# One step of a hybrid streaming encoder: a new order of mixer and last stage, and activations laid out by groups of four tiles

## The chip, the cores and the metric

The kernel runs on one core of one Trainium2 chip. The metric is device time in microseconds (us), the median of several executions. The engines of a core are TensorE (PE), VectorE (DVE), ScalarE (ACT), GpSimd (POOL) and SyncE (SP), which here only issues DMAs. Each runs its own instruction stream in order and waits on semaphores.

## What is computed

640 tokens (512 of a prompt, 8 streams of 16), model width 1024, float32:

```
h  = rmsnorm(x, norm1_g)
cb, cc, ch, q, k, v, rg, ga, gb = split(h @ w_in)        # w_in: 1024 x 9216
u  = cc * ch;  y_conv = cb * conv3(u)                    # causal, width 3
q, k = rope(q), rope(k) / 16                             # 4 heads of 256
o  = chunkwise_retention(q, k, v, state)                 # decay by head
y_ret = silu(rg) * rms_group_norm(o)
x  = x + (sigmoid(ga) * y_conv + sigmoid(gb) * y_ret) @ w_out
h2 = rmsnorm(x, norm2_g)
# PEER: 8 heads, 128 x 128 experts, top 16 of each head
s  = scores of h2 @ wq against two sets of 128 sub-keys; top 16 of each, top 16 of the sums
x  = x + sum over picked experts e: softmax(s_e) * gelu(u_tab[e] . h2) * v_tab[e]
y  = rmsnorm(x, final_g)
```

The outputs are y, the last two rows of u, and the new retention states.

## The kernel before, in words

Tokens lie in five tiles of 128 (`TT`). Products in full accuracy are made of three matmuls: each operand is split in a high part (ACT, `high_a`, L684) and a low part (POOL, `low`, L636).

*Start.* SP loads x; for each tile ACT squares and sums it (`norm_row`, L705), takes the square root (L708), DVE makes the factor with six small operations (`row_factor`, L973 to L978), ACT scales (`scale_rows`, L716), PE transposes (`turn_rows`, L1522), DVE and POOL split the result (`split_rows` L995/L996, `rows_low` L645). All this goes tile by tile.

*Mixer.* `w_in` comes in 72 column tiles through a ring of four buffers (`tile_in`, L460). PE's `product` (L1485 to L1487) makes 128 x 640 outputs with 48 matmuls of 320 columns. ACT copies them out (`out_of_psum`, L699). Tiles come in rounds of 8: four heads (q, q, k, k, v, v, rg, rg), then 8 of gb, then 8 conv rounds of 4 (cc, ch, cb, ga). Beside the round of head h runs the retention of head h - 1: PE's `retention_step` after each product (transposes L1534, scores L1541, outputs L1593, prompt state L1602, then `stream` for 8 streams, L1550 and L1560, the mean square L1617). DVE does `scores` (L1041, the kw products L1047), `rotate_q` and `rotate_k` (L1009 to L1014), `prompt_state` (L1069), `stream_state` (L1078), `outputs` (L1089 to L1099). In the gb round `gb_times` (L1104) stands in place of the rotations.

*Transposed table.* Beside the mixer the 128 tiles of `u_t` are loaded into two buffers (`turn_in`, L479), transposed by DVE (`turn`, L1022) and stored as `u_rows` (`turn_out`, L473). `turn_in(m)` waits until tile m - 2 is transposed. Written-out lists fix where these stand: `EARLY` and `TURN_IN` on SP, the `turn(...)` calls on DVE. SP issues weight tiles, u tiles, u rows and states in one order, and a waiting instruction holds back all behind it.

*w_out.* `by_token` (L1506 to L1508) adds eight parts into each of ten accumulators of 512 columns. Part i waits for the high and low mixer tile i (`m_ready`, set by L1203).

*Queries, up.* 48 query products (L1667), then 128 `up` tiles (L1707): the 384 tokens of the last three tiles (`TD`) against all 16384 experts, GELU by ACT (L872), stored to `acts` in DRAM, 1.5 KB per partition and tile. DVE does the retrieval and makes gates, which go to DRAM as `gates` by groups of four tiles. The first two token tiles go another way: for each of 256 token rows POOL gathers rows of `u_rows` and `peer_v` (L671; 14 slots), and DVE makes dots (L1346) and sums (L1364) in pairs (`pair_step`).

*Last stage (down).* For each group of four tiles SP loads gates and activations (`group_in`, L591 and L593) into two alternating buffers, and tiles of `peer_v` (`down_in`, L604) into a ring of eight. DVE multiplies (`weigh`, L1398), PE multiplies with the value tile: `down` (L1768), or for three of five tiles (`three(e)`) `down_three` (L1760 to L1762), which needs high parts by ACT (L935, L937) and low parts by DVE (`low_of_tile` L1405, `low_of_gated` L1411). In before, `low_of_gated(e - 1)` stands behind `weigh(e)`. At the end the five tiles are normed and stored.

Of the kernel before, what the change touches and what calls it, by code (L numbers as in the profile page):

```python
# [53 lines left out]
UP_BANKS = 2  # L54
AHEAD = 2
# [14 lines left out]
EARLY = 5  # L70
TURN_IN = (3, 3, 2, 3, 2, 2, 2, 1)
# [118 lines left out]
def build_program(nc, io):  # L190
    ctx = ExitStack()
    with ctx:
# [158 lines left out]
        acts = nc.dram_tensor("acts", [NKEY, P, TD], F32).ap()  # L351
# [43 lines left out]
        c_used = sem("c_used")  # L395
        m_ready = sem("m_ready")
# [58 lines left out]
        def _(sp):  # L455
# [34 lines left out]
            for u in range(GROUP):  # L490
                tile_in(u, io["w_in"][GROUP + u, :, :], 1)

# [89 lines left out]
            def group_in(g):  # L582
# [9 lines left out]
                src = acts[g * GROUP:(g + 1) * GROUP, :, :].rearrange("k p t -> p k t")  # L592
                sp.dma_start(al[:, g % 2, :, :], src).then_inc(al_loaded[g % 2], 16)  # L593
# [84 lines left out]
        def _(act):  # L678
# [126 lines left out]
            def conv_tile(ct, u, first=False):  # L805

                if u == 0 and not first:
                    act.wait_ge(c_used, ct)
                out_of_psum(c_in[:, u, :], u % 2, ACT.Sigmoid if u == 3 else ACT.Copy, ct * GROUP + (HEADS * 8 + KT + u))

            def conv_tiles(ct, first=False):
                for u in range(GROUP):
                    a = ct * GROUP + (HEADS * 8 + KT + u)
                    high_a((u + 2) % GROUP, a + 2, a + 2)
                    if first and u == 0:

                        act.wait_ge(gate_used, KT)
# [140 lines left out]
        def _(dve):  # L958
# [9 lines left out]
            def row_factor(which, tt):  # L968


                dve.wait_ge(rms_ready, which * TT + tt + 1)
                r_, t_, m_ = (t[:, tt:tt + 1] for t in (rstd, rms, ss))
# [5 lines left out]
                then(nc.vector.tensor_tensor(r_, r_, t_, ALU.mult), factor_ready, which * TT + tt + 1)  # L978
# [20 lines left out]
            for tt in range(TT + 1):  # L999
                if tt < TT:  # L1000
                    row_factor(0, tt)
                if tt:
                    split_rows(0, tt - 1, hf, g1)
# [29 lines left out]
            def scores(g, r):  # L1033
# [4 lines left out]
                for j in range(PT + 1):  # L1038
                    dve.wait_ge(att_done, g * 5 + (j + 1))
# [4 lines left out]
                    if j == 4:  # L1044
                        turn(0, 1, r, PER_HEAD)
                for s in range(PT):
                    then(nc.vector.tensor_scalar(kw[:, s, :], kv[:, s, 0:DK], key_decay(g, s), None, ALU.mult),  # L1047
                         kw_ready, g * 12 + (s + 1))
# [5 lines left out]
                turn(1, 2, r, PER_HEAD)  # L1054
# [59 lines left out]
            def head_round(h, first):  # L1114
# [24 lines left out]
            for t in range(4):  # L1139
                gb_times(t)  # L1140
                turn(n_gb + 3 + t, 1)
# [699 lines left out]
```

## Time and profile before

| what | us |
|---|---|
| median of three runs | 2345.77 |
| lowest, highest | 2332.7, 2359.89 |
| the profiled execution, its own time | 2338.41 |
| its span | 2336.6 |

Busy times are sums over one engine. "Idle" is time before an instruction in which its engine did nothing, with the name of what released it. The granted clock is TensorE's, as a share of full speed. Stages by the start of PE's work: products 33 to 713, w_out to 780, queries to 932, up to 1692 (gates beside it from 1466), down 1697 to 2328.

### The profile page before, as it was taken

How to read it: one execution, taken by the hardware profiler on the slowest of the kernel's cores; microseconds unless marked ns; L12 is line 12 of the kernel's file. 1: busy time of each engine (PE TensorE's matmuls, PEld its weight loads, DVE VectorE, ACT ScalarE, POOL GpSimd, SP SyncE). 2: the span in 40 equal slices, each digit the busy share in tenths (PEclk: the TensorE clock that was granted, in tenths of full speed). 3: DMA queues.
4: the chain of work that ended last, by engine and by line, in shares of the span. 5: the costliest groups of instructions: out<-in, count | busy, mean ns of one | idle time of the engine just before them, and what ended most of it. 6: DMA issues, size and time to landing. Idle time of an engine off the chain costs nothing.

```text
span 2336.6 us, 30091 instructions
## 1 busy us (share of the span) xinstructions
PE 2228.0 (95%) x10245; PEld 1663.9 (71%) x10245; DVE 1701.5 (73%) x3158; ACT 536.7 (23%) x1087; POOL 802.4 (34%) x606
## 2 busy tenths in 40 slices
PE   6999999899999999999999999999999999999998
PEld 5889989899997975655565655777655656656654
DVE  4576675567755287889979989988576777667676
ACT  3212222122222111121211211333222222122222
POOL 4322122123332005474564655111043343334340
PEclk9999999999999999999999999999999999999999
DMA  4898989989862459899999999787899999999993
GB/s 148 280 334 282 318 275 308 320 298 319 299 215 102 148 181 371 311 394 408 366 412 385 384 412 377 252 281 254 282 392 359 375 386 365 372 387 351 350 409 124
DMA packets 326436, 735.36 MB, mean 315 GB/s; under 512 B 30368, under 2 KB 179616, under 8 KB 326304
## 3 DMA queue, kind: packets, MB, share of 16 engines
q1 hardware_dynamic: 202080, 439.67, 52.5%
q0 software_dynamic: 73728, 268.47, 29.9%
q10 hardware_dynamic: 50496, 25.59, 3.6%
q8 instruction: 67, 1.10, 0.2%
q14 instruction: 65, 0.53, 0.1%
HBM read 604.04 MB, written 129.57 MB: 314 GB/s over the span
## 4 chain that ended last, share of the span: by engine, by line
PE 74%; DMA 12%; DVE 8%; issue 2%; SPq 2%; ACT 1%; POOL 0%; ACTq 0%; DVEq 0%; POOLq 0%
PE ps L1707 27%; PE ps L1768 8%; DMA b<-acts 8%; PE ps L1667 6%; PE ps L1485 5%; PE ps L1487 5%; PE ps L1486 5%; PE ps L1722 4%; PE ps L1760 3%; DMA b<-in_u_t 3%; PE ps L1762 3%; PE ps L1761 3%; PE ps L1560 1%; DVE b L1022 1%; PE ps L1550 1%
## 5 line engine op out<-in xcount | busy, mean ns | idle before, releaser
L1707 PE MATMUL ps<-b,b 128*128 128x384 f32 x2048 | 665.6, 486 | 0.0
L1707 PEld LDWEIGHTS ps<-b,b 128*128 128x128 f32 x2048 | 387.1, 190 | 263.1
L671 POOL DMA_INDIRECT b<-u_rows,b x256 | 255.1, 996 | 848.4 <-DVE b L1346 645.1
L671 POOL DMA_INDIRECT b<-in_peer_v,b x256 | 339.2, 1325 | 114.3 <-DVE ps L1364 66.9
L1485 PE MATMUL ps<-b,b 128*128 128x320 f32 x1152 | 366.0, 318 | 5.0 <-ACT b L699 4.4
L636 POOL TENSOR_TENSOR b<-b,b 128x1024 fp32r<-128x1024 f32 x80 | 195.3, 2445 | 490.5 <-ACT b L684 486.0
L1486 PE MATMUL ps<-b,b 128*128 128x320 f32 x1152 | 359.9, 312 | 0.0
L1487 PE MATMUL ps<-b,b 128*128 128x320 f32 x1152 | 359.7, 312 | 0.0
L1364 DVE SCALAR_TENSOR_TENSOR ps<-b,b,ps 128x1024 f32<-128x1024 f32 x252 | 323.2, 1283 | 46.2 <-ACT b L888 27.3
L1346 DVE CUSTOM_DVE_ANT_0 b<-b,b 128x1024 f32<-128x1024 f32 x256 | 312.4, 1220 | 21.3 <-DMA b<-u_rows,b 19.8
L1768 PE MATMUL ps<-b,b 128*128 128x512 f32 x648 | 286.1, 592 | 0.0
L1022 DVE STREAM_TRANSPOSE b<-b 128x1024 f32<-128x1024 f32 x128 | 157.3, 1239 | 168.4 <-DMA b<-in_u_t 163.5
L1760 PE MATMUL ps<-b,b 128*128 128x512 f32 x444 | 197.0, 444 | 37.8 <-DVE b L1411 37.7
L1485 PEld LDWEIGHTS ps<-b,b 128*128 128x128 f32 x1152 | 220.2, 191 | 6.5 <-issue 5.6
L1486 PEld LDWEIGHTS ps<-b,b 128*128 128x128 f32 x1152 | 220.0, 191 | 0.9
L1487 PEld LDWEIGHTS ps<-b,b 128*128 128x128 f32 x1152 | 219.6, 191 | 0.0
L1768 PEld LDWEIGHTS ps<-b,b 128*128 128x128 f32 x648 | 122.9, 190 | 135.1 <-issue 131.1
L1398 DVE TENSOR_TENSOR b<-b,b 128x384 f32<-128x384 f32 x128 | 71.8, 561 | 188.7 <-DMA b<-acts 172.7
L1762 PE MATMUL ps<-b,b 128*128 128x512 f32 x444 | 177.8, 400 | 0.0
L1761 PE MATMUL ps<-b,b 128*128 128x512 f32 x444 | 177.7, 400 | 0.0
L872 ACT ACTIVATE b<-ps 128x384 f32<-128x384 f32 x128 | 62.6, 489 | 486.2 <-PE ps L1707 480.0
L699 ACT ACTIVATE b<-ps 128x640 f32<-128x640 f32 (+1 forms) x72 | 50.7, 704 | 451.3 <-PE ps L1487 403.4
(158 smaller groups left out, 2585.8 us busy)
## 6 DMA issues: line engine op xcount, KB each, us to landing
b<-in_u_t SPq DMA_DIRECT2D x256, 512.0 KB, 6.1
u_rows<-b SPq DMA_DIRECT2D x512, 128.0 KB, 4.4
b<-in_peer_v SPq DMA_DIRECT2D x128, 512.0 KB, 8.9
b<-in_w_in SPq DMA_DIRECT2D x72, 512.0 KB, 5.5
b<-in_wq SPq DMA_DIRECT2D x48, 512.0 KB, 4.5
acts<-b SPq DMA_DIRECT2D x128, 192.0 KB, 7.8
gates<-b ACTq DMA_DIRECT2D x12, 2048.0 KB, 8.1
b<-gates SPq DMA_DIRECT2D x32, 768.0 KB, 9.6
```

The costliest lines, as they stand in the source:

```text
L636: nc.gpsimd.tensor_tensor(lo[u][:, :], raw[:, u, :], hi[u][:, :].bitcast(F32), ALU.subtract).then_inc(lo_ready, 1)
L671: nc.gpsimd.indirect_dma_start(slots[n % SLOTS][:, :], None, u_rows if kind == "u" else v_rows, bass.IndirectOffsetOnAxis(ap=row_id[:, r_ ...
L1346: nc.vector.tensor_tensor_reduce(up_row, up_row, h_row[:, r_ // P, :], 1.0, 0.0, ALU.mult, ALU.add, dots[:, r_ // PAIR % LINES, r_ % PAIR: ...
L1364: nc.vector.scalar_tensor_tensor(out, down_row, row_w[:, b % LINES, i:i + 1], had, ALU.mult, ALU.add).then_inc(row_done, 1)
L1485: nc.tensor.matmul(out, wa_hi[u][:, cols], h_hi[:, k, tok], start=(k == 0), stop=False)
L1486: nc.tensor.matmul(out, wa_hi[u][:, cols], h_lo[:, k, tok], start=False, stop=False)
L1487: last = nc.tensor.matmul(out, wa_lo[u][:, cols], h_hi[:, k, tok], start=False, stop=(k == KT - 1))
L1707: last = nc.tensor.matmul(ps[:, 2 + e % UP_BANKS, 0:TD], w[:, k * P:(k + 1) * P], h2[:, k, SD:T], start=(k == 0), stop=(k == KT - 1))
L1760: nc.tensor.matmul(out, p_hi[:, u, tok], v_hi[n][:, cols], start=(e == 0), stop=False)
L1761: nc.tensor.matmul(out, p_hi[:, u, tok], v_lo[n][:, cols], start=False, stop=False)
L1762: last = nc.tensor.matmul(out, p_lo[:, u, tok], v_hi[n][:, cols], start=False, stop=False)
L1768: last = nc.tensor.matmul(ps[:, 2 + 2 * i + dh, :], p32[:, e % GROUP, i * P:(i + 1) * P], w[:, dh * 512:(dh + 1) * 512], start=(e == 0), s ...
```

## The change

1. Start: all five tiles are squared first, one square root and one set of factor operations serve all, then the tiles are scaled.
2. The u tiles: 4 early ones are issued before the ninth weight tile instead of 5 behind it, and the lists on SP and DVE are new. In `scores` the kw products and two transposes come before the fourth score.
3. PE: of the 8 streams some stand between the halves of a product.
4. Conv: ACT waits for `cc_used` (cc and ch) and `c_used` (cb and ga) apart, and not for `gate_used`.
5. w_out: the first two accumulators take parts 0 to 6 side by side before part 7.
6. Last stage: `group_in(g + 1)` before the group's `down_in`, `low_of_gated(e)` in its own tile.
7. `acts` has the shape of a group: a partition's four tiles adjoin, so that a group is read in runs of 6 KB.

```diff
-EARLY = 5
-TURN_IN = (3, 3, 2, 3, 2, 2, 2, 1)
+BESIDE = 2
+EARLY = 4
+TURN_FIRST = (4, 2, 3, 2, 2, 2, 2, 1)
+TURN_IN = (2, 0, 2, 3, 4, 1, 3, 3)
...
-        acts = nc.dram_tensor("acts", [NKEY, P, TD], F32).ap()
+        acts = nc.dram_tensor("acts", [NE_GROUPS, P, GROUP, TD], F32).ap()
...
+            sp.wait_ge(xs_ready, TT)
+            for i in range(EARLY):
+                turn_in(i, first=True)
...
-                    if first and t == 0:
-                        sp.wait_ge(xs_ready, TT)
-                        for i in range(EARLY):
-                            turn_in(i, first=True)
-                    for i in range(TURN_IN[t]):
-                        n = sum(TURN_IN[:t]) + i
-                        turn_in(EARLY + n, 0 if first else h - 1, PER_HEAD)
+                    share = TURN_FIRST if first else TURN_IN
+                    for i in range(share[t]):
+                        turn_in(EARLY + sum(share[:t]) + i, 0 if first else h - 1, PER_HEAD)
...
-                    for j in ((3, 4), (5,), (6,), (7, 8))[u]:
+                    for j in ((2, 3), (4,), (5,), (6, 7))[u]:
...
-                sp.dma_start(tile_of(acts, e), spill[:, e % 2, :]).then_inc(a_stored[e % 2], 16)
+                sp.dma_start(acts[e // GROUP, :, e % GROUP, :], spill[:, e % 2, :]).then_inc(a_stored[e % 2], 16)
...
-                src = acts[g * GROUP:(g + 1) * GROUP, :, :].rearrange("k p t -> p k t")
-                sp.dma_start(al[:, g % 2, :, :], src).then_inc(al_loaded[g % 2], 16)
+                src = acts[g, :, :, :].rearrange("p k t -> p (k t)")
+                sp.dma_start(al[:, g % 2, :, :].rearrange("p k t -> p (k t)"), src).then_inc(al_loaded[g % 2], 16)
...
                 if g + 1 < NE_GROUPS:
+                    group_in(g + 1)
                     for u in range(GROUP):
                         down_in((g + 1) * GROUP + u)
-                    group_in(g + 1)
...
-                norm_row(0, tt)
-                if tt:
-                    scale_rows(0, tt - 1, xs)
-            high_a(0, 0, 0, False)
-            scale_rows(0, TT - 1, xs)
+                nc.scalar.activation(ps[...], x[:, tt, :], ACT.Square, accum_out=ss[:, tt:tt + 1]).then_inc(sum_done, 1)
+            act.wait_ge(sum_done, TT)
+            nc.scalar.activation(rms[:, :], ss[:, :], ACT.Sqrt, bias=eps[:, 0:1], scale=1.0 / D).then_inc(rms_ready, TT)
+            for tt in range(TT):
+                scale_rows(0, tt, xs)
+                if tt == 1:
+                    high_a(0, 0, 0, False)
...
-                if u == 0 and not first:
-                    act.wait_ge(c_used, ct)
+                if u in (0, 2) and not first:
+                    act.wait_ge(cc_used if u == 0 else c_used, ct)
...
-                        act.wait_ge(gate_used, KT)
...
                 for j in range(PT + 1):
+                    if j == 3:
+                        for s in range(PT):
+                            then(nc.vector.tensor_scalar(kw[:, s, :], ...), kw_ready, g * 12 + (s + 1))
+                        turn(0, 2, r, PER_HEAD)
...
-                    if j == 4:
-                        turn(0, 1, r, PER_HEAD)
-                for s in range(PT):
-                    then(nc.vector.tensor_scalar(kw[:, s, :], ...), kw_ready, g * 12 + (s + 1))
...
-                turn(1, 2, r, PER_HEAD)
...
                 rotate_q(h)
-                turn(3, 2, h, PER_HEAD)
+                turn(2, 2, h, PER_HEAD)
                 rotate_k(h)
                 prompt_state(g, first)
-                turn(5, 1, h, PER_HEAD)
-                for s in range(STREAMS):
+                stream_state(g, 0)
+                done = 4
+                for s in range(1, STREAMS):
                     stream_state(g, s)
-                    turn(6 + s, 1, h, PER_HEAD)
+                    n = 2 if s in (3, 5, 7) else 1
+                    turn(done, n, h, PER_HEAD)
+                    done += n
...
-            for t in range(4):
-                gb_times(t)
-                turn(n_gb + 3 + t, 1)
+            gb_times(0)
+            turn(n_gb + 2, 1)
+            gb_times(1)
+            turn(n_gb + 3, 1)
+            gb_times(2)
+            turn(n_gb + 4, 1)
+            gb_times(3)
             prompt_state(HEADS - 1, False)
-            turn(n_gb + 7, 1)
...
                 if three(e):
                     low_of_tile(e)
-                if e and three(e - 1):
-                    low_of_gated(e - 1)
+                    low_of_gated(e)
...
+                    if hv == 0:
+                        between()
...
+                for i, pair in parts[:-1]:
+                    ready(i)
+                    for n in range(BESIDE):
+                        add(n, i, pair)
+                ready(e_)
+                for n in range(10):
+                    if n >= 4:
+                        pe.wait_ge(acc_added, stage * 10 + (n - 3))
+                    for i, pair in parts if n >= BESIDE else parts[-1:]:
+                        last = add(n, i, pair)
...
-                for s in {4: range(2), 5: range(2, 5), 6: range(5, 8)}.get(t, ()):
+                for s in {4: (0, 1), 5: (3,), 6: (5,)}.get(t, ()):
                     stream(g, s)
...
+            def streams_inside(g, t):
+                for s in {5: (2,), 6: (4,), 7: (6, 7)}.get(t, ()):
+                    stream(g, s)
```

## Rows read from the trace of the kernel before

**Rows 1.** The page, part 1: busy us, share of span, instructions of each engine.

```profile
PE 2228.0 (95%) x10245; PEld 1663.9 (71%) x10245; DVE 1701.5 (73%) x3158; ACT 536.7 (23%) x1087; POOL 802.4 (34%) x606
```

**Rows 2.** Windows by stage; columns: stretch, length, busy, clock, DMA share, GB/s.

```profile
0.00:60.00 60.00, 37.18 (x204) 33.76 (x205) 24.14 (x52) 22.67 (x31) 25.68 (x20) 1.00 0.42 154
60.00:500.00 440.00, 409.32 (x2575) 385.24 (x2574) 272.24 (x295) 97.57 (x132) 91.78 (x38) 0.96 0.89 299
932.00:1466.00 534.00, 534.00 (x1726) 319.44 (x1725) 489.17 (x1109) 99.15 (x303) 296.00 (x252) 1.00 1.00 382
1697.00:2300.00 603.00, 570.40 (x1913) 367.22 (x1914) 434.28 (x597) 139.49 (x308) 238.60 (x206) 0.98 0.95 368
...
1820.00:1880.00 60.00, 56.98 (x195) 36.32 (x195) 44.58 (x64) 14.91 (x33) 26.50 (x24) 1.00 1.03 409
```

**Rows 3.** Waits of PE over the whole span: us, times, longest.

```profile
PE ps L1760 <- DVE b L1411: 37.7, 14, 5.4
PE ps L1560 <- DVE b L1069: 16.5, 4, 8.8
...
PE ps L1485 <- ACT b L699: 4.4, 1, 4.4
PE ps L1506 <- DVE b L1203: 4.4, 1, 4.4
PE ps L1534 <- ACT b L737: 4.2, 1, 4.2
PE ps L1541 <- DVE b L1041: 2.8, 1, 2.8
```

**Rows 4.** Windows just behind waits: first of six, 723, first of five.

```profile
112.50:119.00 6.50, 6.50 (x16) 3.73 (x16) 2.40 (x3) 2.00 (x4) 1.90 (x1) 0.63 0.87 291
...
723.00:730.00 7.00, 6.93 (x20) 5.55 (x21) 0.69 (x1) 0.00 (x0) 0.00 (x0) 0.62 0.03 9
...
1774.00:1782.00 8.00, 7.88 (x21) 5.93 (x22) 8.00 (x12) 1.74 (x3) 3.46 (x3) 0.65 0.98 367
```

**Rows 5.** Last stage: timeline of VectorE at tile 7; its longest wait, 1697 to 2300.

```profile
1732.24 0.56 DVE L1398 TENSOR_TENSOR b<-b,b 128x384 f32<-128x384 f32 x1 [11.60 <-DMA b<-acts]
1732.71 0.55 DVE L1411 TENSOR_TENSOR b<-b,b 128x384 fp32r<-128x384 f32 x1
...
DVE b L1398 <- DMA b<-acts: 153.5, 23, 11.6
```

**Rows 6.** Timeline: VectorE in round 2; PE's waits for L1069, rounds 1 and gb.

```profile
220.94 0.29 DVE L1041 TENSOR_TENSOR b<-ps,b 128x128 f32<-128x128 f32 x1 [7.06 <-PE ps L1541]
...
223.08 3.17 DVE L1047 TENSOR_SCALAR b<-b,b 128x256 f32<-128x256 f32 x4
...
241.25 1.25 DVE L1022 STREAM_TRANSPOSE b<-b 128x1024 f32<-128x1024 f32 x1 [2.41 <-DMA b<-in_u_t]
...
157.50 1.10 PE L1560 MATMUL ps<-b,b 128*128 128x256 f32 x4 [0.75 <-DVE b L1069]
...
444.64 1.62 PE L1560 MATMUL ps<-b,b 128*128 128x256 f32 x3 [8.83 <-DVE b L1069]
```

**Rows 7.** Timeline of PE: first w_out matmul, first of its last part.

```profile
713.50 0.50 PE L1506 MATMUL ps<-b,b 128*128 128x512 f32 x1 [0.79 <-ACT b L699]
...
723.07 0.77 PE L1506 MATMUL ps<-b,b 128*128 128x512 f32 x1 [4.42 <-DVE b L1203]
```

**Rows 8.** DMA issues, page part 6: KB each, us to landing.

```profile
b<-gates SPq DMA_DIRECT2D x32, 768.0 KB, 9.6
b<-acts SPq DMA_DIRECT2D x32, 768.0 KB, 14.5
```

**Rows 9.** Timeline, first 62 us: ACT scaling tiles 2 and 3, VectorE's first u transpose.

```profile
17.22 1.15 ACT L716 ACTIVATE b<-b,b 128x1024 f32<-128x1024 f32 x1 [2.51 <-DVE b L978]
...
22.16 1.15 ACT L716 ACTIVATE b<-b,b 128x1024 f32<-128x1024 f32 x1 [2.43 <-DVE b L978]
...
59.66 2.43 DVE L1022 STREAM_TRANSPOSE b<-b 128x1024 f32<-128x1024 f32 x2 [24.58 <-DMA b<-in_u_t]
```

More of the change, by code:

```diff
@@ L395, in build_program @@
         c_used = sem("c_used")
+        cc_used = sem("cc_ch_used")
         m_ready = sem("m_ready")
@@ L966, in _, with row_factor @@
             nc.vector.memset(eps[:, :], EPS).then_inc(eps_ready, 1)
-            def row_factor(which, tt):
-                dve.wait_ge(rms_ready, which * TT + tt + 1)
-                r_, t_, m_ = (t[:, tt:tt + 1] for t in (rstd, rms, ss))
+            def row_factor(which, tt, n=1):
+                dve.wait_ge(rms_ready, which * TT + tt + n)
+                r_, t_, m_ = (t[:, tt:tt + n] for t in (rstd, rms, ss))
                 line.then(nc.vector.reciprocal(r_, t_))
@@ L977, in row_factor @@
                 line.then(nc.vector.tensor_scalar(t_, t_, -0.5, 1.5, ALU.mult, ALU.add))
-                then(nc.vector.tensor_tensor(r_, r_, t_, ALU.mult), factor_ready, which * TT + tt + 1)
+                nc.vector.tensor_tensor(r_, r_, t_, ALU.mult).then_inc(factor_ready, n)
+                dve.wait_ge(factor_ready, which * TT + tt + n)
             def split_rows(which, tt, hf_, gain):
@@ L998, in _ @@
             dve.wait_ge(consts, 16 * 2)
[L999 to L1003, printed above, removed]
+            row_factor(0, 0, TT)
+            for tt in range(TT):
+                split_rows(0, tt, hf, g1)
             def rotate(h, src, dst, n):
@@ L1173, in conv_round @@
                 line.then(nc.vector.tensor_tensor(ub[:, 2:2 + PROMPT], cc[:, 0:PROMPT], ch[:, 0:PROMPT], ALU.mult))
-                line.then(nc.vector.tensor_tensor(uv[:, :, 2:], streams_of(cc[:, PROMPT:T]), streams_of(ch[:, PROMPT:T]), ALU.mult))
+                nc.vector.tensor_tensor(uv[:, :, 2:], streams_of(cc[:, PROMPT:T]), streams_of(ch[:, PROMPT:T]),
+                                        ALU.mult).then_inc(cc_used, 1)
+                dve.wait_ge(cc_used, ct + 1)
                 line.then(nc.vector.tensor_copy(uv[:, :, 0:2], sconv[:, ds(ct, 1), :].rearrange("p o (b s) -> p (o b) s", b=STREAMS)))
@@ L1470, in _, with product @@
         def _(pe):
-            def product(u, par, n, a, wait_evac=True, rows_from=None):
+            def product(u, par, n, a, wait_evac=True, rows_from=None, between=lambda: None):
                 pe.wait_ge(lo_ready, n + 1)
@@ L1493, in by_token, with add @@
                 between = list(between)
-                for n in range(10):
+                parts = list(enumerate(zip(lhs, rhs)))
+                e_ = len(parts) - 1
+                def add(n, i, pair):
                     tt, dh = n // 2, n % 2
-                    if not (first and n < 4):
-                        pe.wait_ge(acc_added, stage * 10 + (n - 3))
                     out = ps[:, acc_bank(n, odd), :]
@@ L1501, in by_token @@
                     cols = slice(dh * 512, (dh + 1) * 512)
-                    for i, ((lh, ll), (rh, rl)) in enumerate(zip(lhs, rhs)):
-                        e_ = i == len(lhs) - 1
-                        if n == 0:
-                            ready(i)
-                        nc.tensor.matmul(out, lh[:, tok], rh[:, cols], start=(i == 0), stop=False)
-                        nc.tensor.matmul(out, ll[:, tok], rh[:, cols], start=False, stop=False)
-                        last = nc.tensor.matmul(out, lh[:, tok], rl[:, cols], start=False, stop=e_)
+                    (lh, ll), (rh, rl) = pair
+                    nc.tensor.matmul(out, lh[:, tok], rh[:, cols], start=(i == 0), stop=False)
+                    nc.tensor.matmul(out, ll[:, tok], rh[:, cols], start=False, stop=False)
+                    return nc.tensor.matmul(out, lh[:, tok], rl[:, cols], start=False, stop=(i == e_))
+                for i, pair in parts[:-1]:
[8 more added lines that the diff above has]
+                        last = add(n, i, pair)
                     last.then_inc(acc_done, 1)
@@ L1527, in _, with head_tile @@
                 turn_rows(0, tt, xs)
-            def head_tile(h, t, first=False):
-                product(t % GROUP, t % 2, h * 8 + t, h * 8 + t, not (first and t < 2), 0 if first and t == 0 else None)
+            def head_tile(h, t, first=False, between=lambda: None):
+                product(t % GROUP, t % 2, h * 8 + t, h * 8 + t, not (first and t < 2), 0 if first and t == 0 else None,
+                        between)
             def turn_kv(tt):
```

43 lines of the change are left out of this document (25 added, 18 removed).

## The prediction

> **What bounds the kernel now.** I read the page's engine shares first [rows 1]: TensorE (PE) is busy 2228.0 of 2336.6 us, so all idle time of PE together is 108.6 us. This caps what a reordering can give, apart from the clock. The stage windows [rows 2] say where it lies: 22.8 us in the first 60, 30.7 between 60 and 500 (retention heads), nothing in the up stage (534 of 534 busy), 32.6 in the last stage from 1697 to 2300. The list of PE's waits [rows 3] names what ends it: 37.7 us, 14 times, on `low_of_gated` of VectorE (L1411); 16.5 on `prompt_state` (L1069); 4.4 on ACT's copy out of PSUM (L699); 4.4 on the last low part of the mixer's product (L1203); 4.2 on L737; 2.8 on L1041. To each longer wait belongs a second price [rows 4]: the granted clock falls to its half level (1.2 of 2.4 GHz), and PE's next matmuls run there. Busy time times (1 - clock) is that loss: the first of six between 112 and 500 costs 6.5 x 0.37 = 2.4, the six 2.4, 1.7, 2.0, 2.6, 1.9 and 1.6, sum 12.2; the one at 723 costs 2.7; of five in the last stage the first costs 2.8, the others 1.7 each, sum 9.6.
>
> **Last stage: what the change removes.** The pattern repeats 13 times [rows 5]: tile 7 is the last of its group and one of the `three` tiles. VectorE has its v_lo by 1720, then goes to `weigh(8)`, which waits 11.60 us for the DMA of the next group's activations; only behind it stands `low_of_gated(7)` (L1411), for which PE waits. Two edits hit this, each enough by itself. First, `low_of_gated(e)` comes before `weigh(e + 1)`. It now waits for ACT's p_hi (about 0.5 us of ACT), beside which VectorE's 1.21 us of v_lo runs, so I charge 0; at worst 0.5 a tile, with VectorE busy 434 of 603 us [rows 2], which its lead of three tiles absorbs. Second, `group_in(g + 1)` leaves SP before the four `down_in` of that group. These wait until PE is through tile 4g - 1; the group's own wait (`p_ready`) is met about four tiles earlier. PE needs about 4.4 us a tile (561 over 128, below), so the load starts some 17 us earlier, against VectorE's waits for it of 11.6 at most once the stage runs [rows 5]. What queues behind SP's wait are four value tiles; they keep five tiles, 22 us, to land.
>
> The layout alone: the activations' DMA takes 14.5 us from issue to landing, the gates' of equal size, already in 6 KB runs, 9.6 [rows 8]. Both leave together, so the gap of 4.9 is in part queueing; the layout gives 0 to 4.9 us of latency a group, hidden now either way. The stores keep their runs.
>
> Ideal gain: waits 37.7 - 5.4 (the first, at 1697, where the stage waits for its first loads and not for the order) = 32.3, plus 9.6 of clock, plus 0.5 at the start (L1411 one `weigh` earlier) = 42.4. What may take it back is DMA: 368 GB/s x 603 us = 222 MB at a share of 0.95. In 561 us they need 396 GB/s. The kernel shows 409 for 60 us, and 382 with PE never idle in the up stage [rows 2]. At 409 the bytes take 543 us and PE stays the bound; at 382 they take 581, and 22 is gained. I take **34**, nearer to the ideal since 409 was reached in this very stage.
>
> A rule speaks against this: the Trainium skill, "DMA: Bandwidth & Descriptors" (Specifications), gives about 358 GB/s as the HBM limit of a core. By it these bytes need 620 us and this part would gain nothing. The 409 of [rows 2] is above it, so the measurement decides, and I give it only part of the DMA rival.
>
> **Heads.** PE waits for `prompt_state` 8.8 us in the gb round and 0.75 in round 1 [rows 6]; the list's 16.5 [rows 3] leaves 6.9 for rounds 2 and 3. In front of it VectorE still transposes for `u_rows`, and one transpose waits for its own load (2.41 us). After: the four kw products (3.2 us) and two transposes (2.4) stand between scores 2 and 3, where VectorE now idles 7.06 us [rows 6]; four transposes instead of five precede `prompt_state`, in the gb round five instead of seven. `rotate_k` then waits only for its tile. That is what round 1 shows already, with a stall of 0.75 [rows 6]. So 6.9 falls to 1.5, and their clock cost (4.6) goes; 8.8 + 1.9 go. Gain 5.4 + 4.6 + 10.7 = 20.7, bounds 8 and 22.
>
> Round 1 (4.2 + 2.8, clock 4.1): ACT's copy waits because weight tiles queue in SP behind transposes; VectorE got its first u tile only at 59.66, after 24.58 us of idling [rows 9], since SP issued it after the ninth weight tile. Now it is issued after the eighth, one product or about 7 us earlier (PE's 24 x 2 matmuls at about 0.145), more than either wait. Gain 11.1, bounds 4 and 11.1. The first conv tile (4.4 + 1.6): ACT no longer waits for `gate_used`, gain 6.0, bounds 3 and 6. PE's other, short waits in the heads stay. The streams moved into and behind the products are the same matmuls; where VectorE is late, two adjacent streams wait one 0.7 us operation, -2 at worst. `cc_used` splits a wait that PE does not feel in the conv rounds: 0, bounds 0 and 1.
>
> Sum 37.8. Against it: DMA share is 0.89 over 440 us [rows 2], and the same bytes in 402 us make 0.97. I hold 6 back and take **32** (bounds 13 and 38).
>
> **w_out.** PE had 21 matmuls to issue before `m_ready(8)`, 713.50 to 718.65, then waited 4.42 [rows 7]. With BESIDE = 2 it has 42, at 0.235 each 9.9 us, to 723.4, past the 723.1 at which the product comes. The wait and 2.7 of clock go: 7.1, I take **7** (bounds 4 and 7).
>
> **Start.** One square root and one set of six factor operations for all tiles replace five. They stand in the chain from one scaled tile to the next, 4.94 us (17.22 to 22.16) [rows 9]. Without them I estimate 3.3, so 1.6 saved for each of four tiles. But no scaling starts until the fifth x tile has landed and been squared; four squares, each about the 1.15 us of a scaling of the same size, come first, some 5 us. GpSimd's `low`, 2.4 us, now slows the chain too. 6.4 - 5 - 2.4 is -1, and bare arithmetic is no better than that here: I take **0** (bounds -3 and +3). What stands behind PE's end stays.
>
> **Sum.** 34 + 32 + 7 + 0 = 73. The profiled execution took 2338.4 us (span 2336.6): 2265. The three plain runs have a median of 2345.8, 7 above, and spread over 27; I give two thirds of the 7: **2270 us**.
>
> **Rivals.** A: DMA becomes the bound of the last stage. For it: share 0.95 now, 1.03 in a stretch. Against it: GpSimd's row loads have 14 slots of slack. The stage gains 22 or, at the 375 GB/s near today's mean, 11: 2282 to 2293. B: the u transposes stay bound by their loads in the heads (share 0.97), and stalls come back at other places; 32 falls to 13: 2289. Both together 2305. C, slower: SP stands at `p_ready` before `group_in(g + 1)` with four value tiles behind it. If VectorE is late (rows of retrieval between the weighs), these are late for PE in every group. It decides where `weigh` trails so far that more than the 22 us are used; to lose over 1% it must eat 73 and 24 more, 3.2 us in each of 31 groups. 3.5 each gives 2378. Against it: VectorE is free over a quarter of the stage. D: the stalls merely move, since PE then waits for p_ready of the next group's first tile: the change doesn't do what it says in the last stage; only 39 come from the rest: 2306.
>
> Chances: forecast 0.60, A 0.14, B 0.11, A with B 0.05, D 0.05, C 0.05. All but C, and half of D and of A with B by noise, lie over 1% below 2345.8. A measurement of this kernel tells about 1% from no change. So faster 0.88, within 1% 0.07, slower 0.05. Range: the ideal terms (42 + 38 + 7 + 3 = 90) give 2248; up to A with B, 2308.
>
> **What would show it.** PE's wait on L1411 falls from 37.7 to under 10, VectorE's on the acts DMA from 153.5 to under 35; the last stage is 590 to 602 long instead of 630, at over 385 GB/s. L1069 ends waits of under 4 us in all; no wait on L1203 over 1; the first u transpose is near 53. Wrong if the last stage stays over 620 us, if PE waits there on weight or value DMAs, or if the mixer ends (first w_out matmul) later than 690.

## The result, and the profile after

| | us |
|---|---|
| before, median of 4 runs measured beside the changed kernel (lowest, highest) | 2349.89 (2332.70, 2359.89) |
| after, median of 4 runs | 2273.33 (2269.06, 2288.35) |
| ratio, with its 95% interval | 0.9693 (0.9617 to 0.9769) |
| the profiled execution of after, its own time | 2269.06 |
| forecast, range | 2270, 2248 to 2308 |

The total is as forecast; its parts are not. Stage lengths from the start of PE's first instruction in each stage, in the profiled executions:

| stage | before | after | difference | forecast |
|---|---|---|---|---|
| start | 33.6 | 32.9 | -0.7 | 0 |
| mixer | 679.9 | 663.8 | -16.1 | -32 |
| w_out | 66.5 | 59.6 | -6.9 | -7 |
| queries | 152.8 | 151.2 | -1.6 | none |
| up | 764.4 | 765.3 | +0.9 | none |
| last stage | 630.4 | 585.4 | -45.0 | -34 |
| behind PE's end | 9.0 | 9.1 | +0.1 | 0 |
| span | 2336.6 | 2267.3 | -69.3 | -73 |

The mixer gave half of its term (15.9 us less than forecast) and the last stage a third more (11.0 more). The two errors largely cancel, so that the total came so near is in part luck.

From the page of after, the engines' busy times and the chain that ended last. PE's share was 2228.0 us of a longer span [rows 1]; it is now 97%.

```profile
span 2267.3 us, 30061 instructions
...
PE 2207.6 (97%) x10245; PEld 1653.6 (73%) x10245; DVE 1689.2 (75%) x3134; ACT 538.3 (24%) x1083; POOL 806.9 (36%) x606
...
PE 87%; DVE 4%; DMA 4%; issue 3%; POOL 1%; SPq 1%; ACT 1%; another core or an unknown queue 0%; ACTq 0%; DVEq 0%; POOLq 0%
PE ps L1735 28%; PE ps L1796 12%; PE ps L1695 6%; PE ps L1500 5%; PE ps L1499 5%; PE ps L1501 5%; PE ps L1788 5%; PE ps L1790 5%; PE ps L1789 5%; PE ps L1750 4%; DMA b<-in_u_t 3%; POOL b L638 1%; PE ps L1519 1%; PE ps L1520 1%; PE ps L1521 1%
```

The chain of before, by engine and by line:

```profile
PE 74%; DMA 12%; DVE 8%; issue 2%; SPq 2%; ACT 1%; POOL 0%; ACTq 0%; DVEq 0%; POOLq 0%
PE ps L1707 27%; PE ps L1768 8%; DMA b<-acts 8%; PE ps L1667 6%; PE ps L1485 5%; PE ps L1487 5%; PE ps L1486 5%; PE ps L1722 4%; PE ps L1760 3%; DMA b<-in_u_t 3%; PE ps L1762 3%; PE ps L1761 3%; PE ps L1560 1%; DVE b L1022 1%; PE ps L1550 1%
```

Before, the read of the activations was 8% of the chain; after, it is no longer in the list. The loads of the u tiles were 3% and still are.

What PE waits for in after: line waited for, us in total, times, longest.

```profile
PE ps L1546 <- ACT b L718: 15.5, 1, 15.5
PE ps L1559 <- DVE b L1094: 15.3, 3, 5.8
PE ps L1788 <- DVE b L1426: 5.6, 1, 5.6
PE ps L1546 <- DVE b L1002: 5.1, 8, 1.3
PE ps L1566 <- DVE b L1050: 3.8, 1, 3.8
```

The first row, 15.5, belongs to the start (ACT scaling the first tile): there, in before, PE waited 11.1 us for ACT and 11.2 for the split, now 15.5 and 5.1. L1426 is `low_of_gated`, L1411 in before. Its 14 waits [rows 3] are one, the stage's own start. `prompt_state` (16.5 before) is down to 0.7, and the waits on ACT's copy (4.4), on L737 (4.2) and on the last low part of the product (4.4) are gone. But the second row is new in size: before, PE waited 2.6 us for that line (the last operation of the retention's mean square, L1091 there); now it is 15.3, once each at the start of rounds 2 and 3 and of the gb round (5.8, 5.8 and 3.7).

The stages as windows of after, to be read beside [rows 2]: us, busy time of PE, PEld, DVE, ACT and POOL, granted clock, DMA share, GB/s.

```profile
60.00:500.00 440.00, 420.19 (x2675) 398.97 (x2674) 271.95 (x295) 105.26 (x139) 97.67 (x41) 0.97 0.92 304
907.00:1440.00 533.00, 532.63 (x1719) 318.10 (x1718) 489.30 (x1109) 98.81 (x302) 298.28 (x252) 1.00 1.00 384
1673.00:2230.00 557.00, 557.00 (x1910) 360.74 (x1911) 436.83 (x596) 140.64 (x308) 240.98 (x206) 1.00 0.99 398
```

In the last stage PE has no idle time in 557 us, while the DMAs move 398 GB/s: PE is full and no DMA wait of PE is left. By the Trainium skill, "DMA: Bandwidth & Descriptors" (Specifications), a core's HBM limit is about 358 GB/s; the same page (Bandwidth) has about 358 as what each core gets when both cores of an HBM domain stream, and more for a core alone. The measurement, 398, agrees with the second statement, and not with the first as a limit for this one-core kernel.

**The new wait, in the rows.** VectorE around 280 us in after (start, duration, line, operation, in brackets the idle time before it and its releaser), then PE's instruction that waited.

```profile
280.19 1.25 DVE L1026 STREAM_TRANSPOSE b<-b 128x1024 f32<-128x1024 f32 x1 [5.80 <-DMA b<-in_u_t]
281.36 0.71 DVE L1081 SCALAR_TENSOR_TENSOR b<-b,b,ps 128x512 f32<-128x512 f32 x1
282.85 1.25 DVE L1026 STREAM_TRANSPOSE b<-b 128x1024 f32<-128x1024 f32 x1 [0.79 <-DMA b<-in_u_t]
285.51 1.25 DVE L1026 STREAM_TRANSPOSE b<-b 128x1024 f32<-128x1024 f32 x1 [1.41 <-DMA b<-in_u_t]
286.68 4.11 DVE L1092 RECIPROCAL b<-b 128x640 f32<-128x640 f32 x1
290.82 2.04 DVE L1093 TENSOR_TENSOR b<-b 128x640 f32<-128x640 f32 x1
292.89 0.82 DVE L1094 SCALAR_TENSOR_TENSOR b<-ps,b 128x640 f32<-128x640 f32 x1
```

```profile
293.86 0.87 PE L1559 MATMUL ps<-b,b 128*128 128x128 f32 x3 [5.79 <-DVE b L1094]
```

A transpose for `u_rows` waits 5.80 us for its load and holds the last `stream_state` (281.36), then two more transposes, each with a late load (0.79 and 1.41), hold the reciprocal (286.68). Behind it come 7 us of arithmetic on PE's path. In all VectorE lost 8.0 us to loads here, and PE waited 5.79. The granted clock falls behind these waits to 0.76, 0.71 and 0.54 over some 6 us (1.5, 1.8 and 2.9 us lost), so this one line costs 12.7 us more wait than before and 6.2 of clock: 18.9.

### The profile page after: what moved, and what is told of

It is laid out like the page before. It is cut to its first block, busy times and chain, and to the rows that moved or that the text cites. A ratio compares the mean times of both kernels' runs of the same rounds, so it can differ in the third digit from the quotient of the medians.

```text
span 2267.3 us, 30061 instructions
## 1 busy us (share of the span) xinstructions
PE 2207.6 (97%) x10245; PEld 1653.6 (73%) x10245; DVE 1689.2 (75%) x3134; ACT 538.3 (24%) x1083; POOL 806.9 (36%) x606
## 4 chain that ended last, share of the span: by engine, by line
PE 87%; DVE 4%; DMA 4%; issue 3%; POOL 1%; SPq 1%; ACT 1%; another core or an unknown queue 0%; ACTq 0%; DVEq 0%; POOLq 0%
PE ps L1735 28%; PE ps L1796 12%; PE ps L1695 6%; PE ps L1500 5%; PE ps L1499 5%; PE ps L1501 5%; PE ps L1788 5%; PE ps L1790 5%; PE ps L1789 5%; PE ps L1750 4%; DMA b<-in_u_t 3%; POOL b L638 1%; PE ps L1519 1%; PE ps L1520 1%; PE ps L1521 1%
## 5 line engine op out<-in xcount | busy, mean ns | idle before, releaser
L1796 PE MATMUL ps<-b,b 128*128 128x512 f32 x648 | 286.1, 592 | 0.0
L1788 PE MATMUL ps<-b,b 128*128 128x512 f32 x444 | 194.7, 438 | 5.6 <-DVE b L1426 5.6
L1789 PE MATMUL ps<-b,b 128*128 128x512 f32 x444 | 174.2, 392 | 0.0
L1790 PE MATMUL ps<-b,b 128*128 128x512 f32 x444 | 174.1, 392 | 0.0
```

Of the source, the lines that this page charges most:

```text
L1788: nc.tensor.matmul(out, p_hi[:, u, tok], v_hi[n][:, cols], start=(e == 0), stop=False)
L1789: nc.tensor.matmul(out, p_hi[:, u, tok], v_lo[n][:, cols], start=False, stop=False)
L1790: last = nc.tensor.matmul(out, p_lo[:, u, tok], v_hi[n][:, cols], start=False, stop=False)
L1796: last = nc.tensor.matmul(ps[:, 2 + 2 * i + dh, :], p32[:, e % GROUP, i * P:(i + 1) * P], w[:, dh * 512:(dh + 1) * 512], start=(e == 0), s ...
```

## Experiments on the last stage

Here and below the stage lengths are the main reading. The reason is the up stage, in which no edit changes more than where the activations are stored: over all profiled executions of this study it was 764 to 767 us long in five and 776 to 789 in nine. Of the totals only those of several runs are given with an interval.

Each stage length is of one profile. How far a stage varies without an edit to it, the other runs show: the mixer of before was 679.9 to 684.4 us long in five profiles, that of after 663.8 and 662.4; w_out 65.6 to 66.8 in the old order and 59.5 or 59.6 in the new one; the last stage of after 585.1 to 586.5 in seven profiles, that of before 630.4 and 627.6. So before's 679.9 is the shortest of its five, and the mixer's gain is 16 to 22 us rather than exactly 16.1.

**`low_of_gated` in its own tile's step**, in the kernel before:

```diff
                 if three(e):
                     low_of_tile(e)
-                if e and three(e - 1):
-                    low_of_gated(e - 1)
+                    low_of_gated(e)
```

> The kernel before with one edit: low_of_gated(e) stands in tile e and not behind weigh(e + 1). Theory 1 (PE waited only because this product stood behind a weigh that waits for the next group's activations): PE's wait on it falls from 37.7 us to the first one, 5 to 6; the last stage is 588 to 595 long instead of 630.4; VectorE still waits over 100 us for the activations. Theory 2 (the late load is what counts, and the stall moves to the next tile): PE then waits as much before the first tile of each next group, the stage stays over 615. The mixer is as before, 680 +- 3.

**The group's read ahead of the value tiles**, in the kernel before:

```diff
                 if g + 1 < NE_GROUPS:
+                    group_in(g + 1)
                     for u in range(GROUP):
                         down_in((g + 1) * GROUP + u)
-                    group_in(g + 1)
```

> The kernel before with one edit: group_in(g + 1) is issued before the four value tiles of that group. Theory 1 and theory 2 both: VectorE's wait for the activations falls from 172.7 to the one at the stage's start (about 20), PE's on L1411 to 5 to 6, the stage to 585 to 592. Rival (DMA is the bound of this stage at over 390 GB/s): the load is earlier but waits stay on value or row loads, and the stage is over 600. The rival that SP's wait in front of the value tiles starves PE: PE waits on DMAs of peer_v.

**The layout alone**, in the kernel before:

```diff
-        acts = nc.dram_tensor("acts", [NKEY, P, TD], F32).ap()
+        acts = nc.dram_tensor("acts", [NE_GROUPS, P, GROUP, TD], F32).ap()
...
-                src = acts[g * GROUP:(g + 1) * GROUP, :, :].rearrange("k p t -> p k t")
+                src = acts[g, :, :, :].rearrange("p k t -> p (k t)")
```

> The kernel before with one edit: the layout of the activations by group, read in 6 KB runs. If short runs make the load slow: its time from issue to landing falls from 14.5 us to about 10, VectorE's waits for it from 172.7 to 90 or less, PE's on L1411 from 37.7 to 10 to 20, and the stage shortens by 15 to 30 us. If the 4.9 us over the gates' load are queueing behind it: the latency stays over 13, and the stage within 5 us of 630.

**All three in the kernel before:**

> Kernel before with all three edits of the last stage (the low part of the gated tile in its own tile's step, the group's read issued ahead of the value tiles, activations by group of four in DRAM), its heads and its w_out stage untouched. Each of the three alone left a last stage of 593.2, 586.2 and 596.7 us, the whole change one of 585.4. Theory, each removes the same stalls and the three don't add up: last stage 584 to 588 here, one PE wait of 5 to 7 us at its start, mixer 678 to 685 and w_out 66 to 67 as before, so the last stage's 45 us don't need the new order of the mixer. Rival, part of the 45 comes from what the mixer or w_out edit leaves behind (the two low parts or the clock at the start): last stage 590 or more.

Measured:

| | last stage, us | PE on `low_of_gated` | VectorE on the acts DMA |
|---|---|---|---|
| before | 630.4 | 37.7, 14 times | 172.7, 24 times |
| `low_of_gated` moved | 593.2 | 7.3, 6 times | 149.8, 23 times |
| read first | 586.2 | 6.7, once | 20.6, once |
| layout alone | 596.7 | 14.8, 10 times | 145.6, 25 times |
| the three together | 585.6 | 5.2, once | 19.4, once |
| after | 585.4 | 5.6, once | 19.7, once |

One wait of 19 to 21 us in the last column, and one of 5 to 7 in the column before it, belong to the stage's first loads. Without the former, before has 153.5 us in 23 waits [rows 5].

The total of the layout alone was 2321.52 us (4 runs), ratio 0.9888 (0.9849 to 0.9927). The first two, one run each, took 2315.81 and 2317.51 us, beside 2350.35 (7 runs) for before, both with a long up stage (778 and 782 us); the three together 2300.24 beside 2343.43. In the last of these the mixer (682.1) and w_out (66.8) are those of before: the 45 us need nothing of the other edits.

VectorE's waits, longest kind first, with `low_of_gated` moved (from 1710 us on, so without the first wait):

```profile
DVE b L1398 <- DMA b<-acts: 129.9, 22, 11.3
```

and with the read issued first, where only the stage's first wait is left:

```profile
DVE b L1398 <- PE ps L1762: 65.1, 42, 3.1
DVE b L1398 <- PE ps L1768: 60.2, 27, 4.6
DVE b L1398 <- DMA b<-acts: 20.6, 1, 20.6
```

These two fences say what 153.5 us of waiting by VectorE were worth. In the first kernel it still waits 129.9 us for the same DMA, and PE waits 7.3 on `low_of_gated`: what PE needs is no longer behind that wait. In the second the wait itself is gone, and VectorE waits for PE, as an engine with time to spare should. Either removes the stall. The layout removes no cause; VectorE's waits are 28.3 us less in sum (from 1700 us on):

```profile
DVE b L1398 <- DMA b<-acts: 125.2, 24, 11.5
```

PE's waits fell with them by 22.9. The run was expected to shorten the stage by 15 to 30 us and to halve VectorE's waits; it gave 33.7 and 16% less (172.7 to 145.6). The trace has no landing time for this read. Worked out from the timelines, from its issue to the `weigh` that had waited for it, the median of the waits longer than 6 us is 15.9 us in before and 13.0 here, so the read lands some 3 us earlier; what part of this is the length of the runs and what part queueing is not shown.

The single edits gave 37.2, 44.2 and 33.7 us, the three together 44.8: they overlap almost wholly.

**The old layout and `BESIDE` = 1 in the kernel after:**

```diff
-BESIDE = 2
+BESIDE = 1
...
-        acts = nc.dram_tensor("acts", [NE_GROUPS, P, GROUP, TD], F32).ap()
+        acts = nc.dram_tensor("acts", [NKEY, P, TD], F32).ap()
```

> The changed kernel with two parts undone that lie in different stages: the old layout of the activations, and BESIDE = 1 (one accumulator of w_out before the last mixer tile). If the new order already hides the loads, the last stage stays within 2 us of 585.4; if the layout's lower DMA cost is what let PE run, it is over 595. w_out is 66 to 67 us long instead of 59.6, with a wait of 4 to 5 us on the last low part and some 3 us of half clock behind it.

The last stage took 586.6 us, 1.2 more than in after and 0.1 above the spread of the new order: with it the layout is worth next to nothing. The total of this one run was 2299.23, with an up stage of 786. w_out took 66.8, which is before's 66.5, and its wait came back:

```profile
PE ps L1519 <- DVE b L1218: 4.4, 1, 4.4
```

So `BESIDE` = 2 is the whole of w_out's gain, in which the wait of 4.4 stands with the clock behind it.

## Experiments on the mixer

**The streams placed as before**, in the kernel after:

```diff
-                for s in {4: (0, 1), 5: (3,), 6: (5,)}.get(t, ()):
+                for s in {4: range(2), 5: range(2, 5), 6: range(5, 8)}.get(t, ()):
...
-                for s in {5: (2,), 6: (4,), 7: (6, 7)}.get(t, ()):
+                for s in ():
```

> The changed kernel with PE's streams where they were before (none between the halves of a product). Theory S (stream 7 now comes 4 to 5 us before the head's end, so that the state update behind it, and the square root that waits for it, are late): the waits of PE on L1094 fall from 15.3 us to 3 or less, and the mixer from 663.8 to 648 to 655. Theory T (the transposes on VectorE ahead of the reciprocal, with late loads, set it, wherever the streams stand): 10 us or more of it stays.

Mixer 671.5 us, 7.7 more than after; total of one run 2298.03. The wait grew, as theory T had it:

```profile
PE ps L1559 <- DVE b L1094: 21.1, 3, 8.0
```

The placing of the streams inside the products is thus a gain (by one profile on each side), and not the cause of the new wait.

**The last three transposes of the streams moved behind the mean square**, in the kernel after:

```diff
-                    n = 2 if s in (3, 5, 7) else 1
+                    n = 2 if s in (3, 5) else 0 if s >= 6 else 1
                     turn(done, n, h, PER_HEAD)
                     done += n
-                outputs(g, lambda: turn(14, 2, h, PER_HEAD))
+                outputs(g, lambda: turn(11, 5, h, PER_HEAD))
```

> The changed kernel with three transposes of each head round (behind streams 6 and 7) moved behind L1094. Theory T: VectorE reaches the reciprocal when the square root is there, the waits on L1094 fall from 15.3 to under 4 us, the mixer by 10 to 17 us with the clock, the time by 0.4 to 0.7%. Theory S: the wait falls by less than half. Rival (the loads are bound by DMA and the stall only moves): new waits of PE on scores or on weights of the same size, mixer within 4 us of 663.8.

```profile
PE ps L1566 <- DVE b L1050: 22.2, 4, 7.6
PE ps L1618 <- DVE b L1050: 4.1, 3, 1.9
PE ps L1559 <- DVE b L1094: 2.8, 3, 1.3
```

The aimed-at wait is gone, 15.3 to 2.8, and a larger one stands at the next thing that PE needs of VectorE, the scores of the next head (L1050), in front of which seven transposes now stand instead of four. The mixer was to become 10 to 17 us shorter by theory T and to stay within 4 us of 663.8 by the rival; it became 17.6 us longer, 681.4 us. Theory T was right on the wait and wrong on its worth, and the rival right that the stall moves. The total was 2302.14 us (4 runs), ratio to before 0.9783 (0.9714 to 0.9853). Both edits together:

> The changed kernel with both edits: streams where they were, three transposes behind L1094. Theory T: as a_turns within 3 us. Theory S: as a_streams. If each is half of it: mixer 645 to 650, below either alone.

Mixer 681.6 us, within 3 us of the edit alone, as theory T had it; L1050 23.4 us, total 2299.04 (4 runs), ratio 0.9786 (0.9726 to 0.9846). Moving the transposes moves the wait.

**The loads of the u tiles left out**, once in after, once in before:

```diff
-                sp.dma_start(u_in[m % 2], tile_of(io["u_t"], r * per + m)).then_inc(u_loaded[m % 2], 16)
+                if first and m < 2:
+                    sp.dma_start(u_in[m % 2], tile_of(io["u_t"], r * per + m)).then_inc(u_loaded[m % 2], 16)
...
-                    dve.wait_ge(u_loaded[i % 2], r * (per // 2 * 16) + 16 * (i // 2 + 1))
+                    dve.wait_ge(u_loaded[i % 2], 16)
```

> The changed kernel without the loads of the u tiles after the first two: the transposes and stores work on the same two tiles, so the rows of the table and the first two token tiles of the output are other numbers. Some 63 MB less are read beside the mixer. If late loads are behind the waits on L1094 and on the first round's score: both are gone or under 1 us each time, and the mixer is 645 to 650. If it is the order alone (streams, square root, reciprocal): waits of 3 us or more stay in each round.

> Kernel before with the loads of the u tiles left out but for the first two (the transposes run on old contents, so the table rows are other numbers; the stores stay). The same was done to the kernel after, where the mixer stage fell from 663.8 to 638.6 us. Theory 1, the new order is worth what the sum said and late loads took half of it back: without loads the difference between the two orders is about 32 us, so this kernel's mixer stage stays near 671 (668 to 675), only 5 to 12 below its 679.9, with the waits on the prompt state (L1069, 16.5) and the other old ones still there. Theory 2, the loads cost both orders the same and the new order is worth 16 with or without them: mixer near 655 (652 to 658). Theory 3, the old waits are themselves late loads passed on: mixer below 648, and the new order is worth under 10 once no load is late. Last stage 630 as before in all.

PE's waits between 60 us and the mixer's end, first after without loads, then before without loads:

```profile
PE ps L1560 <- DVE b L1095: 2.6, 3, 1.2
PE ps L1520 <- ACT b L702: 0.8, 1, 0.8
```

```profile
PE ps L1561 <- DVE b L1070: 9.4, 4, 4.7
PE ps L1486 <- ACT b L700: 4.5, 1, 4.5
PE ps L1535 <- DVE b L1092: 2.6, 3, 1.2
PE ps L1507 <- ACT b L700: 0.8, 1, 0.8
```

| mixer, us | with the loads | without | the loads cost |
|---|---|---|---|
| before | 679.9 | 659.7 | 20.2 |
| after | 663.8 | 638.6 | 25.2 |
| difference | 16.1 | 21.1 | |

The totals, one run each, were 2269.11 and 2325.87 us; the first had an up stage of 787 us, which hides the gain of its mixer. Of the theories for the second run the first (671) and the third (under 648) fall; 659.7 lies just above the second's 652 to 658. The new wait of after comes from the loads: without them the line is back to 2.6. But the old stalls came in good part from the loads as well: `prompt_state` 16.5 to 9.4, and the 4.2 and 2.8 of [rows 3] vanish without any change of order. The new order is worth 21 us without the loads and 16 to 22 with them, and the loads cost both orders 20 to 25 us. Leaving them out takes away more than their lateness: SP's time for issuing them, and a third of the DMA traffic of the mixer (289 and 296 GB/s before the edit, 197 and 204 with it). These runs do not tell the three apart.

## Two attempts to make the loads less late

SP in after around the late transpose at 280.19. Each row is a run of DMA issues.

```profile
266.86 0.37 SPq L482 DMA_DIRECT2D b<-in_u_t  x1
267.33 2.81 SPq L476 DMA_DIRECT2D u_rows<-b  x4
270.40 0.37 SPq L527 DMA_DIRECT2D b<-in_dec  x1
270.97 0.41 SPq L527 DMA_DIRECT2D b<-in_dec_s  x1
271.47 0.38 SPq L527 DMA_DIRECT2D b<-in_gq  x1
272.15 0.33 SPq L463 DMA_DIRECT2D b<-in_w_in  x1
272.67 0.33 SPq L482 DMA_DIRECT2D b<-in_u_t  x1
273.11 2.93 SPq L476 DMA_DIRECT2D u_rows<-b  x4
276.24 0.51 SPq L482 DMA_DIRECT2D b<-in_u_t  x1
```

The buffer of the load at 272.67 was free at 270.49 (a transpose from 269.24, 1.25 long); three tables and a weight tile were issued first. The next buffer was free at 272.25, but the load left at 276.24, behind the four stores of a turned tile, 2.93 us of issue. The first load landed 7.5 us after its issue, where the median of its kind is 5.6.

**Loads in pairs, ahead of the stores and tables**, in the kernel after, rounds 2 to 4 (SP's list for tiles 3 and 4 of the head; the tables go behind tile 4's turns):

```diff
+    [("in", 8), ("in", 9), ("out", 6), ("out", 7), ("in", 10), ("out", 8), ("in", 11), ("in", 12)],
+    [("out", 9), ("out", 10), ("in", 13), ("out", 11), ("in", 14), ("in", 15), ("out", 12), ("out", 13)],
```

> Kernel after, only the order in which SyncE issues things in rounds 2 to 4 of the heads is changed: where VectorE makes two transposes in a row, the two loads that follow them are issued one behind the other and the eight stores behind both (now load, four stores of some 0.7 us each, load, four stores); two loads go ahead of the three tables and of the weight load that stood in front of them; the tables go one tile later. Theory late loads by SyncE's issue order (in the trace of after the load for the transpose at 280.19 went out at 272.67, 2.2 us after its buffer was free, the next one at 276.24, 4 us after): VectorE's waits on u tiles between 60 and 500 us fall from 102.9 to under 85, PE's wait on L1094 from 15.3 to under 8, the mixer stage from 663.8 to 652 to 660, the total 5 to 10 us below after. Rival, the DMA queues' share sets it (0.92 in that stretch): the loads go out earlier and land as late, mixer 662 to 666, the median landing of a u load above 6.5 us in place of 5.6, no change in time. Second rival: the stores, now later, hold VectorE through the ring of three turned tiles, mixer over 666.

```profile
DVE b L1043 <- DMA b<-in_u_t: 97.0, 36, 8.9
...
DVE b L1043 <- DMA u_rows<-b: 22.4, 10, 4.4
```

Theory issue order fails here: PE's wait on the mean square stayed, at 16.4 us. The second rival's mechanism appeared: the transposes now wait for the stores of the ring of three turned tiles (22.4 us, none before), the waits on loads fell only from 102.9 to 97.0, and the mixer stayed at 662.9 us. This lies in the first rival's 662 to 666, but its sign, a median landing above 6.5 us, did not come: it was 5.5. Total 2276.96 (4 runs), ratio to before 0.975 (0.9717 to 0.9783).

**One load earlier, the tables later, no pairs**, in the kernel after:

```diff
-TURN_IN = (2, 0, 2, 3, 4, 1, 3, 3)
+TURN_IN = (2, 0, 2, 4, 3, 1, 3, 3)
...
-                    if t == 3:
+                    if t == (3 if first else 4):
```

> Kernel after, in rounds 2 to 4 of the heads one load of a u tile with its four stores goes ahead of the weight load of tile 4, and the three tables go behind tile 4's turns in place of tile 3's; no pairs of loads, so no store goes later by more than that. Theory issue order: the load that the transpose between streams 6 and 7 waits for goes out some 2 us earlier, that wait falls from 5.8 to 3.5 to 4.5 us in each of two or three rounds, no wait on stores comes (under 2 us in all), PE's wait on L1094 falls from 15.3 to 8 to 13, mixer 656 to 662. Rival, the DMA engines' share (0.92): it lands as late, PE's wait stays at 14 or more and the mixer at 662 to 666. Either way under 8 us of the total.

```profile
PE ps L1560 <- DVE b L1095: 11.8, 3, 5.8
PE ps L1567 <- DVE b L1051: 2.2, 1, 2.2
```

The wait on the mean square fell from 15.3 to 11.8 and the mixer from 663.8 to 658.5 us, both as the theory of issue order had it. But one of the three waits stayed at 5.8, and VectorE's waits on u loads rose from 102.9 to 111.2 us between 60 and 500, so that with one profile here and 662.4 to 663.8 in two of the old list the 4 to 5 us are a hint and not more. The total doesn't show them: 2283.35 us (4 runs), ratio to before 0.9722 (0.9669 to 0.9775), against 0.9693 for after. The profiled execution had one of the long up stages, 789.1. ScalarE (L879, the copy and GELU of an up tile) there, before the two gaps of PE in that stage, at 1187 and 1346:

```profile
1164.82 0.49 ACT L879 ACTIVATE b<-ps 128x384 f32<-128x384 f32 x1 [10.82 <-remote]
1186.35 0.87 ACT L879 ACTIVATE b<-ps 128x384 f32<-128x384 f32 x2 [11.83 <-remote]
1345.00 0.49 ACT L879 ACTIVATE b<-ps 128x384 f32<-128x384 f32 x1 [9.63 <-remote]
```

PE waited there 13.2 us in three waits, since ScalarE did not empty its banks. "remote" means that the trace names no releaser; ScalarE had 41.2 us of such waits in this up stage and 15.4 in that of after. Its waits on the store of activations do not set the two apart (45.3 and 38.3 us). The run without loads has PE's gaps at the same two places (11.7 and 6.6). Why some executions have them and others don't was not tried.

What makes the loads late is not settled. SP's order and its time for issuing (2.2 us in the median for the four stores of a tile), the share of the DMA engines (0.92) and the two buffers all have a part in the rows: between 60 and 500 us in after SP itself waited 88.5 us, in 43 waits, for a buffer to be transposed. A third buffer was not tried. None of the variants was shown faster than the changed kernel.

## Why the prediction was right in sum and wrong in its parts

The mechanisms of the last stage and of w_out were right. The mixer's was right at each place it named and wrong in what it took to stay as it was. The sum came right because a term put too high and one put too low stood against each other, and no step of the prediction foresaw that.

**Last stage, 34 forecast, 45.0 measured.** The reading of [rows 5] held: the wait behind `weigh`, two edits each enough by itself, no DMA wait of PE. The step that failed is the amount held back for DMA. I put 42.4 against bounds of 22 (at 382 GB/s) and took 34. The 382 was read in a stage in which PE was never idle; it was that stage's demand, not a ceiling. Asked for 398, the same queues gave 398, and 404 to 413 in the windows from 1736 to 2126 us. PE's idle time in the stage fell by 32.5 us, to nothing, as put (32.3). The other 12.5 is busy time of PE, 597.9 us before and 585.4 after for the same matmuls: 9.6 of it is the clock term; where the last 3 come from the runs do not settle. I also wrote that the layout's latency is "hidden now either way": true beside the new order (1.2 us), but by itself the layout was worth 33.7, of which the prediction said nothing.

**Mixer, 32 forecast, 16.1 measured.** The edits did what the steps said at their own places: `prompt_state` 16.5 to 0.7, ACT's copy 4.4 to 0, L737 4.2 to 0, the first u transpose at 51.96 instead of 59.66. The step that failed is "PE's other, short waits in the heads stay". The 2.6 us on the mean square became 15.3 and cost 18.9 with the clock, and the 2.8 on the scores did not go but became 3.8. The ideal 37.8, less 18.9, less the 5.5 that the scores of round 1 cost now (3.8 of wait, 1.7 of clock) is 13.4, near the 16.1. Counted from the rows it comes to the same: PE's waits in the mixer were 30.5 us before and are 19.8 after, the clock's cost 12.2 and 7.9, which makes 15.0. Behind it stands a wrong reading of [rows 6]: I saw that a transpose waited 2.41 us for its own load and still counted the stall as one of order. The 6 held back for DMA had the right sign and a third of the size. The streams, priced at "-2 at worst", gained: 7.7 us go without their new places.

**Rivals.** B, loads bind and stalls come back elsewhere, with 13 for the mixer, is what happened there (16.1), though I gave it 0.11 and 0.05 with A. Its price was good; its chance was too small, because the list of VectorE's waits on loads (129.9 us in the heads of before, 24.6 of them for the first u tile) was not among what I weighed. Between 60 and 500 us the other 105.3 are 102.9 in after: the new order did not shorten them. A, C and D did not happen: SP waits for `p_ready` 118.5 us in all, at most 8.5 at once, and no value tile was late.

**w_out, 7 against 6.9**, and the start, 0 against 0.7, came out by their steps. The queries and the up stage moved by -1.6 and +0.9, which was in no step and is less than they vary between runs (151.2 to 159.5 and 764 to 789 us).

**The signs named ahead.** Last stage 590 to 602 us: it was 585.4, better than the range. Over 385 GB/s: 398. L1411 under 10: 5.6. VectorE on the acts under 35: 19.7, all of it ahead of the stage. L1069 under 4: 0.7. L1203 under 1: gone. First transpose near 53: 51.96. The mixer's end not later than 690: 696.7 (32.9 + 663.8). This last sign was the one that failed, and it pointed to the right stage.

## What to carry to other kernels

When a wait on an in-order engine is to be moved off the path, ask first what the waiting instruction itself waits for. If it is an order, as in the last stage, moving it removes the stall, and one edit of several takes most of it or all (37.2 and 44.2 of 44.8 us). If it is a supply that is often late, as the u tiles here, a new order can still gain, but a part of the stall comes back at another place: it did in each of the orders tried here, and only leaving the loads out took the 20 to 25 us away. More supply was not tried. A rate read in a stretch where the consumer was never idle is a demand and no bound.

## What was not expected of the hardware

- The DMA engines kept 398 GB/s over 557 us (share 0.99) with three kinds of traffic, value tiles, groups and gathered rows, and PE never waited for them.
- A store of a quarter of a turned tile costs SP 0.5 to 0.8 us to issue (four in 1.9 to 3.2 us in after, in the median 2.2), a load of four times its bytes 0.37. Per tile of `u_t` SP is busy some 2.6 us with issuing, twice the 1.25 that VectorE takes to transpose it.
- The up stage is 764 to 767 us long or 776 to 789, with nothing changed in it but where it stores. In eight of the nine long ones PE's gaps stand 266 to 284 or 422 to 445 us behind the stage's start, or at both; in one of these eight another stands at 127, and the ninth has its only one at 120. An edit worth 5 us can't be told from this in totals of four runs.
